# A mixture-of-experts kernel: the w_down weights of most experts come as 2 MB transfers with 16 KB runs

## The reference

```python
xb = xt[tok]
gu = xb @ w_gate_up[e] + b_gate_up[e]            # (1024) x (1024 x 2048)
gate = jnp.minimum(gu[:, :D_EXPERT], SWIGLU_LIMIT)
up = jnp.clip(gu[:, D_EXPERT:], -SWIGLU_LIMIT, SWIGLU_LIMIT)
act = (up + 1.0) * gate * jax.nn.sigmoid(SWIGLU_ALPHA * gate)
yb = act @ w_down[e] + b_down[e]                 # (1024) x (1024 x 1024)
return yb * wt.astype(yb.dtype)[:, None]
```

## Time and profile before

| | |
|---|---|
| median of 3 runs | 1305.59 us (1304.23 to 1307.17) |
| profiled execution, its own time | 1307.32 us |
| its span | 1305.6 us, mean granted clock 0.993 |
| TensorE matmul busy | 1259.9 us (97%) |
| VectorE / ScalarE / GpSimd busy | 521.2 / 189.9 / 162.6 us |
| HBM read / written | 432.53 / 23.27 MB, 349 GB/s over the span |
| SP's queue | 76,400 packets, 445.69 MB, 83.8% of 16 engines |

### The profile page before, as it was taken

One profiled execution on the slowest core, in us unless ns is written; L12 is line 12 of the kernel. 1 busy time (PEld: TensorE's weight loads), 2 busy tenths in 40 slices (PEclk: granted clock), 3 DMA queues, 4 the chain that ended last, 5 costly groups with the idle time before them and its releaser, 6 DMA issues.

```text
span 1305.6 us, 52682 instructions
## 1 busy us (share of the span) xinstructions
PE 1259.9 (97%) x21821; PEld 747.6 (57%) x21821; DVE 521.2 (40%) x1733; ACT 189.9 (15%) x437; POOL 162.6 (12%) x267
## 2 busy tenths in 40 slices
PE   7999999999999999999999999999999999988885
PEld 4446654545666665665665665666656656644552
DVE  6454223447333333343343343333433433422337
ACT  3431123332001000000000000010000000000002
POOL 4100330122101101101011011011011010000111
PEclk9999999999999999999999999999999999999998
DMA  6453131619999999999999999999999999999997
GB/s 224 147 193 131 34 130 49 258 65 342 404 421 407 421 410 422 417 420 410 419 416 421 412 422 414 422 417 420 413 416 421 416 421 417 420 421 421 421 425 283
DMA packets 80504, 455.73 MB, mean 349 GB/s; under 512 B 11057, under 2 KB 23018, under 8 KB 30730
## 3 DMA queue, kind: packets, MB, share of 16 engines
q1 hardware_dynamic: 76400, 445.69, 83.8%
q0 software_dynamic: 3888, 8.40, 1.7%
q10 hardware_dynamic: 106, 0.04, 0.0%
HBM read 432.53 MB, written 23.27 MB: 349 GB/s over the span
## 4 chain that ended last, share of the span: by engine, by line
PE 52%; DMA 44%; DVE 2%; issue 1%; SPq 0%; ACT 0%; POOL 0%; POOLq 0%; ACTq 0%; DVEq 0%
DMA ring<-in_w_gate_up_dram 26%; PE ps L1924 18%; DMA ring<-in_w_down_dram 16%; PE ps L1492 11%; PE ps L1976 8%; PE ps L1512 4%; PE ps L1890 3%; PE ps L1553 2%; DMA x_rows_dram<-cat,rowi 1%; PE ps L1916 1%; PE ps L1546 1%; PE ps L1967 0%; DMA ring<-in_x_dram 0%; DMA ring<-x_rows_dram 0%; PE ps L1899 0%
## 5 line engine op out<-in xcount | busy, mean ns | idle before, releaser
L1924 PE MATMUL ps<-ring,cat 128*32 128x256 f32 x9856 | 550.1, 380 | 7.6 <-DMA ring<-in_w_gate_up_dram 7.6
L1924 PEld LDWEIGHTS ps<-ring,cat 128*32 128x32 f32 x9856 | 306.6, 110 | 219.9 <-DMA ring<-in_w_gate_up_dram 10.9
L1976 PE MATMUL ps<-ring,cat 128*32 128x256 f32 x4800 | 276.2, 380 | 13.2 <-DMA ring<-in_w_down_dram 12.6
L1976 PEld LDWEIGHTS ps<-ring,cat 128*32 128x32 f32 x4800 | 142.6, 110 | 118.1 <-DMA ring<-in_w_down_dram 11.3
L1492 PE MATMUL ps<-hbuf,ring 128*128 128x512 f32 x320 | 147.7, 608 | 1.7 <-DVE hbuf L922 1.7
L1313 DVE TENSOR_REDUCE wslot<-ps 128x2 f32<-128x6 f32 x75 | 12.4, 165 | 318.7 <-ACT cat L848 317.1
L606 POOL DMA_INDIRECT pair_rows_dram<-cat,rowi x73 | 72.7, 996 | 432.1 <-ACT cat L848 432.1
L840 ACT ACTIVATE cat<-cat 128x128 f32<-128x128 f32 x154 | 47.7, 309 | 516.8 <-DVE cat L1337 516.8
L1890 PE MATMUL ps<-hbuf,cat 128*32 128x256 bf16 x2432 | 105.2, 273 | 0.6 <-DVE cat L1410 0.6
L1492 PEld LDWEIGHTS ps<-hbuf,ring 128*128 128x128 f32 x320 | 58.9, 192 | 68.2 <-issue 65.8
L1337 DVE TENSOR_SCALAR cat<-ps 128x128 f32<-128x128 f32 x154 | 44.8, 291 | 128.8 <-PE ps L1924 128.7
(11 more groups left out here) (369 smaller groups left out, 818.5 us busy)
## 6 DMA issues: line engine op xcount, KB each, us to landing
ring<-in_w_gate_up_dram SPq DMA_DIRECT2D x256, 1024.0 KB, 10.0
ring<-in_w_down_dram SPq DMA_DIRECT2D x128, 1024.0 KB, 9.9
ring<-in_w_in_dram SPq DMA_DIRECT2D x10, 1024.0 KB, 6.3
pair_rows_dram<-cat SPq DMA_DIRECT2D x4, 2048.0 KB, 10.9
ring<-pair_rows_dram SPq DMA_DIRECT2D x4, 2048.0 KB, 20.6
ring<-in_w_out_dram SPq DMA_DIRECT2D x1, 4096.0 KB, 12.9
ring<-in_x_dram SPq DMA_DIRECT2D x4, 512.0 KB, 5.4
x_rows_dram<-ring SPq DMA_DIRECT2D x2, 1024.0 KB, 9.7
```

The costliest lines, as they stand in the source:

```text
L1924: last = mm(ps[SLOTS * q:SLOTS * (q + 1), banks[half], 0:2 * P].rearrange("p (s m r) -> p s m r", s=2, m=2), x[:, SLOTS * u:SLOTS * (u + 1 ...
L1976: last = mm(ps[SLOTS * q:SLOTS * (q + 1), 1, 0:QD], actT[:, c // 4, SLOTS * (c % 4):SLOTS * (c % 4 + 1)], w[:, i, q * QD:(q + 1) * QD], st ...
```

## The change

The units of gate/up stay as they are. `w_down` is cut in two blocks of 512 rows, of which partition p holds the four consecutive rows 4p to 4p+3 (16 KB). Where two units of `w_down` with numbers n (even) and n + 1 belong to an expert from the third visited to the last but one, one transfer of 2 MB fills both slots, and it raises the semaphore of the first slot alone. In the other experts (the first two and the last) each half of these 16 KB comes as a transfer of its own, with runs of 8 KB. SyncE waits until both slots are free, TensorE waits before either unit for the whole transfer (`arrival`), and the column order of gate/up and of SwiGLU follows the new rows.

```diff
         def quarter(v, q, half):
-            pairs = v.rearrange("p s (m r) -> p s m r", r=2 * P)
-            return pairs[:, :, 2 * half:2 * half + 2, 2 * SLOTS * q:2 * SLOTS * (q + 1)]
+            fours = v.rearrange("p s (m r) -> p s m r", r=4 * P)
+            return fours[:, :, half, P * q:P * (q + 1)]
         def in_order(v):
-            return v.rearrange("p (m i c) -> p m c i", m=2, c=2)
+            return v.rearrange("p (i c) -> p c i", c=4)
         def chunked_half(v):
-            return v.rearrange("p (m c i) -> p m c i", m=2, c=2)
+            return v.rearrange("p (c i) -> p c i", c=4)
...
-            r = 2 * P * (u - NGU)
-            return w_down[0, bass.ds(e, 1), r:r + 2 * P, :].rearrange("a (p c) n -> (a p) (c n)", c=2)
+            r = 4 * P * ((u - NGU) // 2)
+            rows = w_down[0, bass.ds(e, 1), r:r + 4 * P, :].rearrange("a (p c) n -> (a p) (c n)", c=4)
+            return rows[:, u % 2 * UNIT:(u % 2 + units) * UNIT]
+        def unit_dst(slot, units=1):
+            return ring[:, slot * UNIT:(slot + units) * UNIT]
+        def doubled(n):
+            return RING + NU <= n < NU * (E - 1) and n % 2 == 0 and n % NU >= NGU
+        def arrival(n):
+            lead = n - 1 if n % 2 and doubled(n - 1) else n
+            loads = [k for k in range(lead % RING, lead + 1, RING) if not (k % 2 and doubled(k - 1))]
+            return slot_in[lead % RING], 16 * len(loads)
...
                     n = NU * e + u + RING
-                    if n >= NU * E:
+                    if n >= NU * E or n % 2 and doubled(n - 1):
                         continue
-                    landed = n - AHEAD
-                    sp.wait_ge(w_used, used + (u + 1))
+                    units = 2 if doubled(n) else 1
+                    signal, count = arrival(n - AHEAD)
+                    sp.wait_ge(w_used, used + (u + units))
                     if e == 0 and u >= NGU:
                         sp.wait_ge(side_ps, 2 + u + 1 - NGU)
-                    sp.wait_ge(slot_in[landed % RING], (landed // RING + 1) * 16)
-                    load_unit(following[n // NU - e], n % NU, n % RING)
+                    sp.wait_ge(signal, count)
+                    load_unit(following[n // NU - e], n % NU, n % RING, units)
...
             def landed(e, u):
-                slot, turn = slot_of(e, u)
-                pe.wait_ge(slot_in[slot], (turn + 1) * 16)
+                slot, _ = slot_of(e, u)
+                pe.wait_ge(*arrival(NU * e + u))
```

More of the change, by code:

```diff
@@ L310, in chain, with unit_src @@
             return link
-        def unit_src(e, u):
+        def unit_src(e, u, units=1):
             if u < NGU:
                 return w_gate_up[0, bass.ds(e, 1), u * P:(u + 1) * P, :].rearrange("a p c -> (a p) c")
-            r = 2 * P * (u - NGU)
-            return w_down[0, bass.ds(e, 1), r:r + 2 * P, :].rearrange("a (p c) n -> (a p) (c n)", c=2)
-        def unit_dst(slot, u):
-            return ring[:, slot * UNIT:(slot + 1) * UNIT]
+            r = 4 * P * ((u - NGU) // 2)
[9 more added lines that the diff above has]
+            return slot_in[lead % RING], 16 * len(loads)
         def slot_of(j, u):
@@ L378, in _, with load_unit @@
             sp.dma_start(wrt[:, :, :], w_router[0].rearrange("(k p) e -> p k e", p=P)).then_inc(pool_router_in, 16)
-            def load_unit(e, u, slot):
-                sp.dma_start(unit_dst(slot, u), unit_src(e, u)).then_inc(slot_in[slot], 16)
+            def load_unit(e, u, slot, units=1):
+                sp.dma_start(unit_dst(slot, units), unit_src(e, u, units)).then_inc(slot_in[slot], 16)
             load_unit(0, 0, 0)
@@ L1916, in gate_up_bias @@
                         last = mm(ps[SLOTS * q:SLOTS * (q + 1), banks[half], 0:2 * P].rearrange(
-                            "p (s m r) -> p s m r", s=2, m=2), selu[:, :], quarter(bias, q, half), start=start, stop=False)
+                            "p (s r) -> p s r", s=2), selu[:, :], quarter(bias, q, half), start=start, stop=False)
                 last.then_inc(gub_used, 1)
@@ L1924, in gate_up_unit @@
                     last = mm(ps[SLOTS * q:SLOTS * (q + 1), banks[half], 0:2 * P].rearrange(
-                        "p (s m r) -> p s m r", s=2, m=2), x[:, SLOTS * u:SLOTS * (u + 1)],
+                        "p (s r) -> p s r", s=2), x[:, SLOTS * u:SLOTS * (u + 1)],
                         quarter(w, q, half), start=opens and u == 0, stop=u == NGU - 1)
```

## The result

| | before | after |
|---|---|---|
| median of 5 runs | 1305.59 us (1304.23 to 1307.63) | 1314.85 us (1312.72 to 1317.65) |
| ratio | | 1.007, 95% interval 1.0049 to 1.0091 |
| profiled execution, its span | 1307.32, 1305.6 us | 1316.87, 1315.1 us |

The account below looks back on a forecast made before the run. TensorE and the load stream were taken to bound the expert loop at almost one pace. Profiled 1307.3 - 4.2 (stream) + 0.9 (given back) = 1304.0 us, or 1302.3 from the median of 1305.6; range 1299.8 to 1307.0.

Parts of the forecast that it names:

- What bounds the kernel: Expert loop: TensorE and the unit loads run almost at one pace, 61.5 against 61.8 us per two experts.
- The stream: DMA queue's w_down loads: 58 transfers of 2 MB with 16 KB packets were to save 4.2 us, lower end 0.
- by packets: Upper estimate for the load stream: 464 packets of 16 KB, each 13 ns cheaper than two of 8 KB, 6.0 us.
- by rate: Other estimate for the load stream: 426 GB/s against 421, 1.2% of 289 us, 3.4 us saved.
- the rival of small savings: Load stream: longer packets save little, 1.7 us with nothing given back, 1303.9 us; chance 0.12.
- TensorE's waits: Down product waits for a whole pair: a shift of 0.86 us, once and not per expert.
- SyncE's waits: Slot wait of every second expert: pair issued up to 0.86 us later; 0.9 us of gain given back as idle queue.
- the queue's reserve: Data still queued ahead at SyncE's slot waits: 0.7 us at 419.5 and 1.4 at 913.9, set against 0.86 of delay.
- The slower one: Slot waits: later pair issue empties the queue, 1308.3 us with eight of 13 places, 1312.6 with all; chance 0.14.
- Layout and scatters: Gate/up column order and VectorE's PSUM step cost zero; scatters landing up to 2.4 us later stay hidden.
- The cut runs: w_down transfers: 16 KB runs might be cut at 8 KB again, 1305.6 + up to 1 us; chance 0.02.

## Why the prediction was wrong

*What bounds the kernel* was right, and so was the arithmetic 61.5 against 61.8 us per two experts. I drew from it that both are near the limit, and not that a loop through both might be near it too. The sums come out as written; what failed is the account of how the waits combine.

*The stream.* The term was 4.2 us, by packets 6.0 and by rate 3.4. Measured where it can show, with short blocks and a deep gate: 3.5 us at best. In the packets of the two runs with a deep gate, 16 KB cost 613 ns against 2 x 312 without those of over 660 and 330; with these it was 621 against 2 x 314, which is 464 x 7 ns = 3 us and not 6. The rate was the better route of the two. With the gate as the change has it the gain was at most 1 us, below even the rival of small savings (1.7 us). The shallower queue behind a pair, which I had called enough ("two units (5 us) still queued"), may be a part of that; how much isn't shown.

*TensorE's waits.* The step that failed is "This is a shift of 0.86 us that occurs once, not per expert." It holds for a stream that runs by its own clock. Here TensorE's later arrival frees the slots later, on which the stream waits at the next expert with two blocks, so the shift comes round again. The landing wait alone costs 5.3 us, not 0.9.

*SyncE's waits.* The price, 0.86 us, and the place were right. I set this delay against the queue's reserve (1.4 us) and TensorE's against nothing; but they are in one loop and add: 1.72 us by rows 3, 1.7 us in the medians of the landings. The reserve that I read from two places was 1.9 us on average over the 11 places of this execution, and 1.25 in that of the kernel with the new order alone; it did not protect the loop in full, since with both waits the units behind came more slowly although something was still queued. So the slack must be taken from the whole loop.

By the changed kernel's 62.85 us per two experts, less 1.72 and plus what the pairs gain (0.2), the loop before took 61.3 us: 0.4 less than the 61.7 of the stream. This sum uses the run that it explains. The three runs with 1 MB transfers give 61.0 (61.89 - 0.86), 61.1 (62.00 - 0.86) and 61.0 (62.68 - 1.72), a slack of 0.6 to 0.7. By that the changed kernel would lose some 0.9 us a round (1.72 - 0.2 - 0.65) and not 1.1; the difference is open. That the two waits are the cause doesn't rest on this sum but on the runs that leave out one or both.

11 rounds of 1.1 us are 12.3 us; this profiled execution entered the stretch 1.4 us earlier and won 0.2 us behind it, which makes the 10.7 us by which its last unit lands later (1277.1 against 1266.5). The 0.9 us that I let the slots give back should have been all of the gain and 9 us more.

*The rivals.* The slower one named half of this mechanism, the later issue of a pair, with the place, 13 places and 0.86 us each, and gave 1308.3 with 8 of them and 1312.6 with all. 1314.85 is beyond it since the landing wait was missing in it. It had 0.14.

*Layout and scatters* at zero: right (ratio 1.0004; blocks of 12.30 us; scatters landed after 6.4 us instead of 6.2). *The cut runs*: excluded by the packets. SP's queue carried 7,936 packets of 16 KB, of which 512 are the pair rows' as before and 7,424 are 58 x 128. The Trainium skill ("DMA: Bandwidth & Descriptors", Anatomy of one DMA) gives its fixed 2.0 us for transfers issued by GpSimd; these are SyncE's. Here it did not show as serial time: 58 transfers fewer gave 3.5 us at best, 60 ns each.

## What to carry to other kernels

Where buffers are handed back and forth, follow each added wait once around: load, landing, use, release, next load. Delays of the consumer and of the producer add in that loop, and the slack to set them against is the loop's, not the one that each wait seems to have. In this kernel a larger transfer was free only where neither its last buffer's release nor its last half's landing comes last. That was one of the two pairs in each expert, and a different one by the number of blocks.

## What was not expected of the hardware

- Leaving out half of the quarters' matmuls (69 instead of 128 in the row of a block's gate/up) left the block at 12.30 us; a quarter of the columns in six of eight units brought gate/up from 7.08 to 3.24 us and the block to 9.55, 0.9 us of it a wait for VectorE. So gate/up's time followed the columns of one quarter of TensorE and not the number of quarters in use. Down products and the rest were not tried.
- Some packets are slow, and more of them at the slot waits. Of the changed kernel's 16 KB unit packets between 360 and 1160 us 4% took over 660 ns, 1.1 us on average; within 4 us before and 8 us behind the issues at the 11 slot waits it was 13%. In the kernel with pairs only where no wait of them comes last it was 0.3% of all. Why is open.
- Six units in flight instead of four gave nothing in the kernel before (ratio 1.0011, 1.0002 to 1.0019), rather a loss of 1 us; with doubled transfers and short blocks perhaps 1 us of gain (0.9982 to 0.9973, intervals that overlap).
